# Gate and up products of 14 of 22 column blocks in Strassen's form, activations by way of DRAM

## What is computed

```python
FFN_HIDDEN = -(-8 * D_MODEL // (3 * 256)) * 256        # 2816, 22 blocks of 128
def swiglu(h, w_gate, w_up, w_down):
    return (jax.nn.silu(h @ w_gate) * (h @ w_up)) @ w_down
...
        h = rmsnorm(x, norm_g[l, 2]) * (1 + sc2) + sh2
        y = swiglu(h, ffn_w_gate[l], ffn_w_up[l], ffn_w_down[l])
        x = x + (1 + g2) * rmsnorm(y, norm_g[l, 3])
```

## Time and profile before

| | us |
|---|---|
| median of 3 runs | 2762.52 (2761.63 to 2764.63) |
| the profiled execution | 2767.59 |
| its span, first to last instruction | 2765.8 |
| TensorE busy | 2614.0 |
| VectorE, ScalarE, GpSimd busy | 1173.4, 1035.3, 1006.2 |
| mean granted clock of TensorE | 0.981 |

### The profile page before, as it was taken

How to read it: one execution, slowest core, us unless ns; L and a number is a source line. 1 busy time by engine, 2 the same in 40 slices (tenths; PEclk the granted TensorE clock), 3 DMA queues, 4 the chain that set the end, 5 groups by cost and what they waited for, 6 DMA issues and landing times.

```text
span 2765.8 us, 34937 instructions
## 1 busy us (share of the span) xinstructions
PE 2614.0 (95%) x12488; PEld 2134.9 (77%) x12488; DVE 1173.4 (42%) x1589; ACT 1035.3 (37%) x1677; POOL 1006.2 (36%) x436
## 2 busy tenths in 40 slices
PE   5999999988999999999999998888999999999997
PEld 3777777777788888888887877776778888888885
DVE  7466655550531055310357536666441015410145
ACT  3354544343432233322333335555443223322222
POOL 0111110103544444444443434343644444444443
PEclk9999999999999999999999999998999999999998
DMA  6232322233223223223325732112222232232223
GB/s 255 69 107 101 114 100 92 92 130 130 92 92 98 95 94 99 93 97 99 123 97 189 261 106 69 68 68 100 91 92 93 98 99 97 93 99 92 98 99 106
DMA packets 92164, 296.32 MB, mean 107 GB/s; under 512 B 9824, under 2 KB 10144, under 8 KB 92064
## 3 DMA queue, kind: packets, MB, share of 16 engines
q1 hardware_dynamic: 92064, 295.00, 31.4%
HBM read 272.95 MB, written 22.02 MB: 107 GB/s over the span
## 4 chain that ended last, share of the span: by engine, by line
PE 53%; issue 26%; POOL 8%; DVE 6%; DVEq 2%; ACT 2%; DMA 1%; SPq 1%; POOLq 0%; ACTq 0%
PE ps L636 10%; PE ps L640 10%; PE ps L637 10%; POOL w_lo L556 8%; PE ps L784 3%; PE ps L971 3%; PE ps L974 3%; PE ps L977 3%; PE ps L750 2%; PE ps L853 2%; PE ps L771 2%; DVEq L1802 2%; DMA arena<-ada_w 1%; PE ps L895 1%; DMA w_raw<-weights 1%
## 5 line engine op out<-in xcount | busy, mean ns | idle before, releaser
L556 POOL TENSOR_TENSOR w_lo<-w_raw,w_hi 128x1024 fp32r<-128x1024 f32 x370 | 903.5, 2444 | 1692.7 <-ACT w_hi L1041 933.5
L636 PE MATMUL ps<-h_hi,w_hi 128*128 128x512 f32 x2184 | 868.6, 398 | 21.1 <-DVE h_lo L1495 8.4
L637 PE MATMUL ps<-h_lo,w_hi 128*128 128x512 f32 x2184 | 857.2, 392 | 0.0
L1041 ACT ACTIVATE w_hi<-w_raw 128x1024 fp32r<-128x1024 f32 x290 | 306.7, 1058 | 663.7 <-PE ps L640 359.7
L640 PE MATMUL ps<-h_hi,w_lo 128*128 128x512 f32 x2184 | 541.0, 390 | 0.0
L636 PEld LDWEIGHTS ps<-h_hi,w_hi 128*128 128x128 f32 x2184 | 414.1, 190 | 124.1 <-DVE h_lo L1495 15.1
L637 PEld LDWEIGHTS ps<-h_lo,w_hi 128*128 128x128 f32 x2184 | 414.3, 190 | 86.7 <-issue 2.4
L640 PEld LDWEIGHTS ps<-h_hi,w_lo 128*128 128x128 f32 x2184 | 411.3, 188 | 85.8
L1920 DVE TENSOR_TENSOR arena<-arena,ps 128x512 f32 (+1 forms) x88 | 60.5, 688 | 778.3 <-PE ps L640 778.3
L1935 DVE TENSOR_TENSOR a_lo<-arena,a_hi 128x512 fp32r<-128x512 f32 x88 | 205.6, 2336 | 206.7 <-ACT a_hi L1424 206.7
L1410 ACT ACTIVATE arena<-ps 128x512 f32<-128x512 f32 x88 | 52.7, 599 | 323.9 <-PE ps L640 323.9
(11 more groups left out here) (207 smaller groups left out, 2577.4 us busy)
## 6 DMA issues: line engine op xcount, KB each, us to landing
w_raw<-weights SPq DMA_DIRECT2D x370, 512.0 KB, 3.4
arena<-ada_w SPq DMA_DIRECT2D x80, 512.0 KB, 3.5
arena<-ada_w SPq DMA_DIRECT2D x8, 1024.0 KB, 14.9
x<-xT SPq DMA_DIRECT2D x4, 2048.0 KB, 13.4
proj<-stage SPq DMA_DIRECT2D x12, 512.0 KB, 3.4
x_d<-x SPq DMA_DIRECT2D x8, 512.0 KB, 4.8
arena<-proj SPq DMA_DIRECT2D x8, 512.0 KB, 3.6
x<-x_d SPq DMA_DIRECT2D x2, 2048.0 KB, 11.8
```

The source lines that it names most:

```text
L556: pool.tensor_tensor(w_lo[:, s, :], w_raw[:, s, :], w_hi[:, s, :].bitcast(f32), ALU.subtract).then_inc(lo_done, 1)
L636: pe.matmul(bank(b), w, high[:, k, :], start=k == 0, stop=False)
L637: pe.matmul(bank(b), w, low[:, k, :], start=False, stop=False)
L1041: a.activation(w_hi[:, slot, :], w_raw[:, slot, :], ACT.Copy).then_inc(hi_done, 1)
```

## The change

In each layer the feed-forward block becomes: eight blocks (16 units, `plain`) for token half 0 as before; then 14 blocks for both halves at once (`strassen`); the down product of half 0; the same eight plain blocks for half 1; the down product of half 1.

In `strassen` two neighbouring blocks of one weight matrix (rows of a 2x2 form), the two halves of the k-blocks (its inner dimension) and the two token halves (its columns) make a 2x2 by 2x2 product, done with seven products in place of eight. A **group** is such a pair of blocks of gate or of up; 14 groups make 98 **products** q, each of 4 k-blocks: 12 matmuls. Four operands are sums of weight quarters (`sum1` to `sum3`, of which `sum2` is written twice; GpSimd), and the other side uses five tiles `T1` to `T4` and `B22` in `comb` made from h of both token halves (`turn` on VectorE, `t_high` on ScalarE, during the plain pairs 3 to 6). `w_hi` and `w_lo` are cut in four slots of 512 columns. VectorE joins the seven products to four results. `mean` of `pre` comes after pair 3 instead of pair 7, and `update` is done in one piece after pair 0. Activations of half 0, and of half 1 for the 14 blocks, are written to DRAM (`act_d`) and read back, four blocks ahead, into `ring` in the down products.

```diff
+PLAIN = 8
+GROUPS = FB - PLAIN
+PRODUCTS = 7 * GROUPS
+FFN_USE = 2 * PLAIN + FB
...
+        act_d = nc.dram_tensor("act_d", [2, FB, P, HALF], f32, kind="Internal").ap()
...
+        a_f = over("a_f", 2048, at_a, f32)[:, :].rearrange("p (s t) -> p s t", s=4)
+        comb = over("comb", 20480, at_arena, f32r)[:, :].rearrange("p (c u k t) -> p c u k t", c=5, u=2, k=KB // 2)
+        T1, T2, T3, T4, B22 = range(5)
+        ring = arena[:, 8192:10240].rearrange("p (s t) -> p s t", s=4)
+        plain_act = arena[:, 4096:8192].rearrange("p (s t) -> p s t", s=PLAIN)
+        sum1, sum2, sum3 = a_f[:, 0, :], a_f[:, 2, :], a_f[:, 1, :]
+        part, part2, part4, gate_sw, act_sw = y3[:, 0, :], a_f[:, 3, :], y3[:, 4, :], [y3[:, i, :] for i in (1, 2, 3, 5)], [y3[:, i, :] for i in (6, 7)]
...
+        def combo_slot(q):
+
+            return (q + 2 * (q >= PRODUCTS // 2)) % 4
...
+                    j, kind = divmod(g, 2)
+                    if g > 1:
+                        sp.wait_ge(sw_free, GROUPS * layer + g - 1)
...
+                def store(j, m):
+                    sp.wait_ge(prod_done, 4 * (GROUPS // 2 * layer + j) + m + 1)
+                    half, block_ = sw_out(j, m)
+                    sp.dma_start(act_d[half, PLAIN + block_], act_sw[m % 2]).then_inc(act_sto[m % 2], 16)
+
+                def rung(half, u):
+
+                    if u > 3:
...
+                    sp.dma_start(ring[:, u % 4, :], act_d[half, act_row(half, u)]).then_inc(act_full[u % 4], 16)
...
+                    def low(c, src):
+                        q = 7 * g + c
+                        pool.wait_ge(sw_hi, PRODUCTS * layer + q + 1)
+                        return pool.tensor_tensor(combo_part(w_lo, q), src, combo_part(w_hi, q).bitcast(f32), ALU.subtract)\
+                            .then_inc(sw_lo, 1)
+
+                    pool.wait_ge(sw_raw[g % 2], (32 if g % 2 else 48) * n)
+                    if g == 0:
+                        pool.wait_ge(free1, T_FFN[layer] + PLAIN)
+                    pool.tensor_tensor(sum1, a21, a22, ALU.add).then_inc(sw_sum, 1)
+                    pool.drain()
+                    if g == 0:
+                        pool.wait_ge(act_std[0], 64 * (layer + 1))
+                    pool.tensor_tensor(sum2, sum1, a11, ALU.subtract).then_inc(sw_sum, 1)
+                    low(0, a11)
+                    low(1, sum2)
+                    low(2, sum1)
+                    if g == 0:
+                        pool.wait_ge(free1, T_FFN[layer] + PLAIN + 1)
+                    pool.tensor_tensor(sum3, a11, a21, ALU.subtract).then_inc(sw_sum, 1)
+                    pool.drain()
+                    low(3, sum3)
+                    low(4, a12)
+                    pool.tensor_tensor(sum2, a12, sum2, ALU.subtract).then_inc(sw_sum, 1)
+                    pool.drain()
+                    low(5, sum2)
+                    low(6, a22)
+                    pool.drain().then_inc(sw_free, 1)
 
             lows(0, USE_OUT[0] + 2)
...
+                for i in range(PLAIN):
+                    for s in range(2):
+                        if half and i < 2:
+                            pe.wait_ge((dn_ev0, dn_ev1)[s], 4 * dn_idx(layer, 0) + i + 1)
+                        pe.wait_ge((free0, free1)[s], tiles + i)
+                        unit(use + 2 * i + s, (use + s) % 2, 2 * (i % 2) + s, h_job(layer, 2, half) if i == s == 0 else None)
+                    if i == 0:
+                        mean(*post[0])
+                    if i == 3 and pre:
+                        mean(*pre)
+
...
+                half4 = lambda t, k0: t[:, k0:k0 + KB // 2, :]
+                moving = [(half4(h_hi, 0), half4(h_lo, 0), 0), (comb[:, T2, 0], comb[:, T2, 1], 4), (comb[:, T1, 0], comb[:, T1, 1], 2),
+                          (comb[:, T3, 0], comb[:, T3, 1], 3), (half4(h_hi, 4), half4(h_lo, 4), 0), (comb[:, B22, 0], comb[:, B22, 1], 1),
+                          (comb[:, T4, 0], comb[:, T4, 1], 5)]
+                for g in range(GROUPS):
+                    G, j = GROUPS * layer + g, g // 2
+                    for c in range(7):
+                        q = 7 * g + c
+                        b = 4 * (g % 2) + (0, 1, 2, 3, 0, 1, 3)[c]
+                        if g == 0 and c < 4:
+                            pe.wait_ge((free0, free1)[c % 2], tiles + PLAIN + c // 2)
+                        elif g == 1 and c == 0:
+                            pe.wait_ge(t_done, 20 * (layer + 1))
+                        elif c == 0:
+                            pe.wait_ge((gate_done, prod_done)[g % 2], 4 * (GROUPS // 2 * layer + j))
+                        elif c == 4:
+                            pe.wait_ge(e_done, G + 1)
+                        elif c == 5:
+                            pe.wait_ge(u2_done, G + 1)
+                        elif c == 6:
+                            pe.wait_ge(u3_done, G + 1)
+                        high, low, order = moving[c]
+                        pe.wait_ge(sw_hi, PRODUCTS * layer + q + 1)
+                        for k in range(KB // 2):
+                            if g == 0 and order:
+                                pe.wait_ge(t_done, 20 * layer + 5 * k + order)
+                            w = combo_part(w_hi, q)[:, k * P:(k + 1) * P]
+                            pe.matmul(bank(b), w, high[:, k, :], start=k == 0, stop=False)
+                            pe.matmul(bank(b), w, low[:, k, :], start=False, stop=False)
+                        pe.wait_ge(sw_lo, PRODUCTS * layer + q + 1)
+                        for k in range(KB // 2):
+                            mm = pe.matmul(bank(b), combo_part(w_lo, q)[:, k * P:(k + 1) * P], high[:, k, :], start=False, stop=k == KB // 2 - 1)
+                        mm.then_inc(sw_done, 1)
+
...
+                        if first and m > 3 and half == 0:
+                            pe.wait_ge(prod_done, 2 * GROUPS * (layer + 1) - 3 + (1, 2, 0, 3)[m - 4])
...
+            def sw_high(layer, q):
+
+                g, c = divmod(q, 7)
+                before = slot_before(q)
+                if before >= 0:
+                    a.wait_ge(sw_done, PRODUCTS * layer + before + 1)
...
+                a.activation(combo_part(w_hi, q), src, ACT.Copy).then_inc(sw_hi, 1)
...
+                    g, c = divmod(q, 7)
+                    if q + 4 < PRODUCTS:
+                        sw_high(layer, q + 4)
...
+            def a_low(layer, half, u):
+
+                v.wait_ge(ah_done, FB * dn_idx(layer, half) + u + 1)
+                v.tensor_tensor(a_lo[:, u % 2, :], act_source(half, u), a_hi[:, u % 2, :].bitcast(f32), ALU.subtract)\
+                    .then_inc(al_done, 1)
...
+                    v.tensor_tensor(small[:, 92:96], mod[:, c + 4:c + 8], mod[:, c:c + 4], ALU.subtract)
+                    second(0)
+                v.scalar_tensor_tensor(b4, x[:, k, HALF:S], gain[:, g:g + 1], bank(7), ALU.mult, ALU.mult)
+                v.drain()
+                v.wait_ge(hf_done, 8 * layer + k + 5)
+                v.scalar_tensor_tensor(b6, b4, shift(0), y3[:, k, :], ALU.add, ALU.subtract).then_inc(t_src, 1)
+                low(1, B22, b5, shift(4))
+                v.wait_ge(t_copy, 4 * layer + k + 1)
+                v.scalar_tensor_tensor(b4, late_copy(k), small[:, 92 + k:93 + k], b4, ALU.add, ALU.subtract).then_inc(t_src, 1)
+                low(2, T1, b6)
+                v.drain()
+                low(3, T3, b4)
+                v.tensor_tensor(b6, b4, y3[:, k, :], ALU.add).then_inc(t_src, 1)
+                if k < 3:
+                    second(k + 1)
+                v.drain()
+                low(4, T2, b6)
+                v.scalar_tensor_tensor(b4, b6, -1.0, y3[:, k + 4, :], ALU.mult, ALU.add).then_inc(t_src, 1)
+                v.drain()
+                low(5, T4, b4)
+                v.drain()
...
+                    if g == 0:
+                        v.wait_ge(act_std[1], 64 * (layer + 1))
+                    v.tensor_tensor(part2, b[1], part, ALU.add).then_inc(u2_done, 1)
+                    v.drain()
+                    v.wait_ge(sw_done, done + 3)
+                    v.tensor_tensor(part4, b[2], part2, ALU.add)
+                    v.drain()
+                    v.wait_ge(sw_done, done + 4)
+                    v.tensor_tensor(b[2], b[3], part4, ALU.add).then_inc(c_done, 1)
+                    v.tensor_tensor(part2, b[3], part2, ALU.add).then_inc(u3_done, 1)
+                    v.drain()
+                    gated(0)
+                    v.wait_ge(sw_done, done + 5)
+                    v.tensor_tensor(b[0], b[0], part, ALU.add).then_inc(c_done, 1)
+                    v.drain()
+                    gated(1)
+                    v.wait_ge(sw_done, done + 6)
+                    v.tensor_tensor(b[1], b[1], part4, ALU.add).then_inc(c_done, 1)
+                    v.drain()
+                    gated(2)
+                    if g == GROUPS - 1:
+                        a_low(layer, 0, 0)
+                    v.wait_ge(sw_done, done + 7)
```

(16 more changed lines are left out.)

331 lines of the change are left out of this document (274 added, 57 removed).

## The result

The changed kernel takes 2697.26 us in the median (2696.61 to 2700.04, 4 runs) against 2762.39 for the kernel before on the same chip (2761.63 to 2764.63, 4 runs): a ratio of 0.976, with an interval of 0.9748 to 0.9772. It is 65.1 us faster. The prediction had 2688.0, so 9.3 us of the forecast gain did not come. The profiled execution took 2696.61 us, with a span of 2694.6.

What follows compares the result with a forecast made beforehand. The prediction took TensorE, full with matmuls at a fixed pitch, to bound the kernel. It summed 2762.5 - 76.2 (matmuls removed) + 1.7 (small slacks) = 2688 us, with a range of 2684.5 to 2706.

Steps and rivals of the forecast that it cites:

- the count and the pitch: Whole feed-forward block: 336 fewer matmuls at an unchanged 0.2267 us each save 76.2 us.
- the steady state: Groups within strassen: 19.04 us each on TensorE, GpSimd's 14.3 us and other engines' work hidden; cost nothing.
- rival B: Strassen groups: feeding by GpSimd at 1.749 us an instruction becomes the bound, 42 to 56 us back; chance 0.07.
- the entry: Plain pairs into strassen: operands ready in time, narrowly, with slacks of 1.5 to 2.9 us; plain pairs end at 88.8.
- the forecast's own mechanism: Whole kernel: matmul saving with nearly everything else hidden, 2685 to 2692 us, chance 0.67.
- rival A: Handover into strassen stalls TensorE, some 5.5 up to 9 us a layer; 2692 to 2708 us, chance 0.18.
- the clock: Strassen: rival that TensorE falls to its lower clock; 14% of matmuls there cost the 76.2 us; chance 0.05.
- Out of strassen ... Even: Strassen into the down product: bank 7 wanted after 1.6 us, VectorE's last add and gate product need 1.5.
- the sentence on DMA: Transfers throughout the changed block: cost nothing, stores wait on SP behind already started products, activation blocks land in 2.7 us.
- the allowance: Seams between stages: 1.7 us added for places where a slack of 1.5 or 0.1 proves too small.

Runs made afterwards that it cites:

- e4: Changed kernel with the third product of every group computed twice, so a group has eight products' matmuls; 2776.25 us.
- e6: Changed kernel with three of GpSimd's seven subtractions in each group done twice; 2729.22 us.
- e7: Changed kernel with five of GpSimd's seven subtractions in each group done twice; 2807.48 us.
- e1: Changed kernel with the first two down weight rows and first four activation loads issued ahead of the last pair of groups' stores; 2700.0 us.
- e3: Changed kernel with only the first four activation loads issued ahead of those stores, the two weight rows still behind; 2699.64 us.
- e8: Changed kernel with VectorE's low part of T3 in the last turn of each layer done seven times; 2707.3 us, one time taken.
- e5: Changed kernel with the first two down weight rows issued ahead of the last pair of groups' stores and the first activation load between them; 2687.56 us.

## Why the prediction was right, and where it was off

**Right: the count and the pitch.** 336 matmuls at 0.2267 are 76.2 us. Strassen lasted 14 x 19.04 us to the hundredth, and e4 gave back 75.3 to 79.0 for them. The Trainium skill (TensorE: Matmul & The Clock Gate, Back-to-back issue gap) gives 216 ns at 512 columns for a lone matmul; the stretches of strassen ran at 226.7.

**Right: the steady state, with less room than said.** TensorE never waited in it. VectorE has 7 adds and, on average, 2 gate products in a group, one instruction more than the 8 of the prediction; that cost nothing. GpSimd's subtractions took 1.283 to 1.311 us in 196 executions, so they were not held, and VectorE's stayed at 0.69. The room was 3.1 us a group and not 4.7, since GpSimd's handovers with ScalarE were left out of its sum. At the 1.749 of rival B a group would, as an estimate, have been 15.9 + 11 x 0.457 = 20.9. B did not happen, but e6 and e7 show its mechanism and its price: 26.9 us for a chain 1.14 over the 19.04, 107.2 for one 3.93 over it.

**Right: the entry.** The plain pairs were to end at 88.8 and ended at 88.6 (823.65 - 735.06); the product of pair 7 was to follow at 91.8 and did (826.82). Timeline of VectorE and then of ScalarE in the kernel after at that place:

```profile
825.94 0.69 DVE L1906 TENSOR_TENSOR comb<-ps,comb 128x512 fp32r<-128x512 f32 x1 [0.67 <-ACT comb L1361]
826.82 0.69 DVE L2342 TENSOR_TENSOR a_f<-a_f,ps 128x512 f32<-128x512 f32 x1 [0.19 <-issue]
```

```profile
821.83 0.62 ACT L1375 ACTIVATE w_hi<-glr 128x512 fp32r<-128x512 f32 x1
...
829.07 0.63 ACT L1375 ACTIVATE w_hi<-a_f 128x512 fp32r<-128x512 f32 x1 [2.65 <-POOL a_f L759]
```

Product 0's high part is begun at 86.8 on the prediction's clock (821.83), where it said 87.3. `sum3`'s copy ends at 94.6 (829.70) against 94.4. So slacks of 1.5 to 3 us, worked out over chains of five handovers from rows of the kernel before, held. The measured 2697.26 lies outside the 2685 to 2692 that the forecast's own mechanism was given, and in the part of the whole range (2684.5 to 2706) that was there for rival A. Rival A's mechanism did not happen: no microsecond was lost at the entry. That the stated range holds the time is luck: a stall at the other seam happened to have the size that was feared at this one.

**Right: the clock.** It stayed at 1.00 with a change of bank every 12 matmuls. The Trainium skill (TensorE: Matmul & The Clock Gate, A second HAM failure mode: psum-queue depth-cycling) would have let one fear otherwise; two stretches of strassen, 266 and 259 us long, show nothing of it. The falls found in e1, e3, e4, e6 and e8 were behind exit stalls.

**Wrong: "Out of strassen ... Even".** This step costed the exit at 0 (with 1.7 for all the small slacks), and it measured 9.4. It looked only at the bank that the first down row takes last, and it took VectorE to be free for it. It did not ask when the row's weights and activations are issued, nor that `a_low`, which needs the activations, stands ahead of VectorE's last add. What it did look at measured 0.33 us at each exit once the loads came early (e5). The same gap is in the sentence on DMA, "all stores wait on SP behind products that TensorE has long started": the harm of a store was not its own wait but the loads that stand behind it on the queue. (A block of activations also took 3.7 us to land in the median, not 2.7; this cost nothing further in the rows behind the first.) With 0 replaced by 9.4 and the allowance dropped, 2762.4 - 76.2 + 9.4 = 2695.6 against 2697.26 measured; the 1.7 left is within the spread of the runs. Taking the stall away gave 2687.56 (e5), the time that the forecast had for the change itself.

## What to carry to other kernels

Where TensorE is full, cutting matmuls pays at their pitch. What it costs is at the seams between stages. So follow at each seam not only the banks but each issuing queue: which waiting instruction stands ahead of the next stage's first loads? When you move such loads forward, look at what falls behind them: in e1 it was a store, and an engine was waiting for its buffer. Move only as many as the next stage's first row needs. An engine's room is its period less its whole chain with handovers, not less its busy time.
